# One matmul for the high and low parts of the last 184 tokens in the first input phase

## The reference

```python
h = rmsnorm(x, norm_g)
proj = jnp.einsum('btd,dc->btc', h, w_in)
xa, za, v, bg, cg, zb, ga, gb = jnp.split(proj, SPLIT_IDX, axis=-1)
ya, new_pool = pool_mixer(xa, pool_buf, offset, w_pool_mix, pool_scale)
ya = ya * jax.nn.silu(za)
yc, new_conv = conv_mixer(cg * v, conv_buf, w_conv)
yb = bg * yc * jax.nn.silu(zb)
merged = (jax.nn.sigmoid(ga + b_gate[:D_MODEL]) * jnp.einsum('bte,ed->btd', ya, w_proj_pool)
          + jax.nn.sigmoid(gb + b_gate[D_MODEL:]) * jnp.einsum('bte,ed->btd', yb, w_proj_conv))
x = x + jnp.einsum('btd,de->bte', merged, w_out)
```

## Time and profile before

| | |
|---|---|
| median of 3 runs | 2417.72 us (2416.65 to 2417.8) |
| span of the profiled execution, first to last instruction | 2415.0 us |
| TensorE (PE) matmul busy | 2392.6 us, 99% |
| TensorE weight loads (PEld) busy | 2332.7 us, 97% |
| VectorE (DVE) busy | 1700.3 us, 70% |
| ScalarE (ACT) busy | 894.0 us, 37% |
| granted TensorE clock, mean | 0.998 of full |

### The profile page before, as it was taken

The page is one execution under the profiler, slowest core; times in us unless marked ns, Lnnn a source line. Parts: engine busy times, 40 slices in busy tenths (PEclk is TensorE's granted clock), DMA queues, the critical chain, the costliest instruction groups (busy, mean ns, idle before and its releaser), DMA issues.

```text
span 2415.0 us, 42738 instructions
## 1 busy us (share of the span) xinstructions
PE 2392.6 (99%) x17842; PEld 2332.7 (97%) x17842; DVE 1700.3 (70%) x2329; ACT 894.0 (37%) x1316; POOL 116.0 (5%) x220
## 2 busy tenths in 40 slices
PE   8999999999999999999999999999999999999998
PEld 7999999999999999999999999999999999888886
DVE  6676666666666586777868777765755887877676
ACT  7333333333333343323322222233533533532535
POOL 3010000000000000000000000000000011100000
PEclk9999999999999999999999999999999999999999
DMA  7563333232323454434433343345645767898656
GB/s 268 198 205 110 107 106 111 99 118 90 127 90 127 163 188 151 150 136 151 150 132 113 136 138 135 107 154 208 227 168 171 275 241 278 296 343 306 243 178 227
DMA packets 196655, 418.06 MB, mean 173 GB/s; under 512 B 12617, under 2 KB 114045, under 8 KB 182448
## 3 DMA queue, kind: packets, MB, share of 16 engines
q1 hardware_dynamic: 170928, 284.85, 35.0%
q0 software_dynamic: 23744, 125.24, 13.7%
q10 hardware_dynamic: 1792, 5.24, 0.6%
HBM read 281.00 MB, written 133.77 MB: 172 GB/s over the span
## 4 chain that ended last, share of the span: by engine, by line
PE 97%; DVE 0%; issue 0%; ACT 0%; DVEq 0%; POOL 0%; POOLq 0%; ACTq 0%
PE ps L1328 76%; PE ps L1475 12%; PE ps L1390 7%; PE ps L1497 1%; PE ps L1543 1%; DVE ops L2195 0%; ACT ops L1683 0%; DVE out L2458 0%; PE ps L1520 0%; DVE out L2511 0%; DVEq L226 0%; DVE h0raw L2612 0%; POOL rstd L1309 0%; ACT squares L1804 0%; ACT squares L1813 0%
## 5 line engine op out<-in xcount | busy, mean ns | idle before, releaser
L1328 PE MATMUL ps<-ops,hi 128*128 128x272 f32 x9728 | 1325.2, 288 | 0.1
L1328 PEld LDWEIGHTS ps<-ops,hi 128*128 128x128 f32 x9728 | 1264.5, 188 | 0.4 <-DVE ops L2195 0.3
L1328 PE MATMUL ps<-ops,lo 128*128 128x272 f32 x4864 | 708.6, 288 | 0.0
L1328 PEld LDWEIGHTS ps<-ops,lo 128*128 128x128 f32 x4864 | 647.4, 188 | 0.0
L1604 ACT ACTIVATE hi<-sb 128x512 fp32r<-128x512 f32 x440 | 278.2, 632 | 576.3 <-PE ps L1328 444.1
L2169 DVE TENSOR_TENSOR pb<-pb,ps 128x544 f32<-128x544 f32 x330 | 237.5, 720 | 261.8 <-PE ps L1328 261.6
L2025 DVE TENSOR_TENSOR lo<-sb,hi 128x512 fp32r<-128x512 f32 x440 | 303.1, 689 | 153.3 <-ACT hi L1604 148.7
L1604 ACT ACTIVATE hi<-raw 128x512 fp32r<-128x512 f32 x264 | 166.8, 632 | 371.6 <-PE ps L1328 357.6
L2025 DVE TENSOR_TENSOR lo<-raw,hi 128x512 fp32r<-128x512 f32 x264 | 181.8, 689 | 103.0 <-ACT hi L1604 103.0
L1475 PE MATMUL ps<-ms_hi,mt 128*128 128x512 f32 x896 | 221.3, 389 | 0.0
L1475 PEld LDWEIGHTS ps<-ms_hi,mt 128*128 128x128 f32 x896 | 168.2, 188 | 34.8
(11 more groups left out here) (173 smaller groups left out, 1580.2 us busy)
## 6 DMA issues: line engine op xcount, KB each, us to landing
raw<-in_w_in_dram SPq DMA_DIRECT2D x156, 512.0 KB, 4.0
pb<-part SPq DMA_DIRECT2D x39, 1088.0 KB, 6.0
part<-pb POOLq DMA_DIRECT2D x37, 1088.0 KB, 5.3
mt_raw<-opq SPq DMA_DIRECT2D x28, 1024.0 KB, 6.3
gates<-pb POOLq DMA_DIRECT2D x16, 1088.0 KB, 8.7
gate<-gates SPq DMA_DIRECT2D x32, 544.0 KB, 6.2
ms<-in_w_out_dram SPq DMA_DIRECT2D x16, 1024.0 KB, 9.5
ops_raw<-opq SPq DMA_DIRECT2D x15, 1088.0 KB, 6.8
```

Source lines behind the costliest of these rows:

```text
L1328: mm = nc.tensor.matmul(ps[b][:, c, 0:HC], w[:, w_slot, kt * P:(kt + 1) * P], operand[:, kt, half, c * HC:(c + 1) * HC], start=fresh and k ...
```

## The change

In the products q = 0 to 6 of pairs 3 to 39 (H0 alone, the half-length L products not), the 544 tokens are no longer cut in two quarters of 272. They are cut in 360 (MAIN) and 184 (REST). For each `kt` and the high weights, two matmuls take the 360 tokens (high part, low part) into the same columns, and one takes the high and the low parts of the 184 tokens side by side, 368 columns, into two neighbouring ranges of the accumulator. For the low weights there is one matmul of 360 and one of 184. The first range of 184 lies right behind the 360, so that the read-out sees 544 columns in a row; the second range is added by a further VectorE instruction, `drain_rest`. All slots so made are now counted in `dve_count`, and waits that had named ScalarE's copy alone name both.

```diff
+    def is_wide(g):
+        return NC < g < FIRST[H1]
+
+    def has_rest(s):
+        g, q = pair_of(s)
+        return is_wide(g) and q < NQ
...
-        if by_dve:
+        if by_dve or has_rest(s):
             nd += 1
             dve_count[s] = nd
...
+        REST = 184
+        MAIN = TH - REST
+        EDGE = 512 - MAIN
...
         def psum(s):
+            if has_rest(s):
+                return flat[bank(s)][:, EDGE:EDGE + TH]
             return ps[bank(s)][:, :, 0:HC]
+
+        def psum_rest(s):
+            return flat[bank(s)][:, EDGE + TH:EDGE + TH + REST]
...
+            def wide_terms(b, w_slot, operand, weights, fresh):
+
+                own = flat[b]
+                pe.wait_ge(w_hi, weights)
+                for kt in range(KQ):
+                    w = hi[:, w_slot, kt * P:(kt + 1) * P]
+                    for half in (0, 1):
+                        nc.tensor.matmul(own[:, EDGE:512], w, operand[:, kt, half, 0:MAIN],
+                                         start=fresh and kt == 0 and half == 0, stop=False, skip_group_check=True)
+                    nc.tensor.matmul(own[:, 512:512 + 2 * REST].rearrange("p (h n) -> p h n", h=2), w,
+                                     operand[:, kt, :, MAIN:TH], start=fresh and kt == 0, stop=False,
+                                     skip_group_check=True)
+                pe.wait_ge(w_lo, weights)
+                for kt in range(KQ):
+                    w = lo[:, w_slot, kt * P:(kt + 1) * P]
+                    nc.tensor.matmul(own[:, EDGE:512], w, operand[:, kt, 0, 0:MAIN], start=False, stop=kt == KQ - 1,
+                                     skip_group_check=True)
+                    mm = nc.tensor.matmul(own[:, 512:512 + REST], w, operand[:, kt, 0, MAIN:TH], start=False,
+                                          stop=kt == KQ - 1, skip_group_check=True)
+                mm.then_inc(product_done, 1)
...
-                    terms(bank(s), s % R, ops[:, q], split_of_slot(s), None, q in (0, 1, 5))
+                    wide_terms(bank(s), s % R, ops[:, q], split_of_slot(s), q in (0, 1, 5))
                     return
...
+            def drain_rest(s):
+                g, q = pair_of(s)
+                if s not in dve_count or not has_rest(s):
+                    return
+                own = target(s)[:, MAIN:TH]
+                if s in act_count and not (in_quad(g) and (g, q) == (first_of(g) + 1, 0)):
+                    dve.wait_ge(act_drained, act_count[s])
+                else:
+                    dve.wait_ge(main_drained, main[0])
+                each = nc.vector.tensor_tensor(own, own, psum_rest(s), ALU.add)
+                if in_quad(g) and q == 4:
+                    own = out_tile(g)[:, 1, MAIN:TH]
+                    each = nc.vector.tensor_tensor(own, own, psum_rest(s), ALU.add)
                 each.then_inc(dve_drained, 1)
...
                 split_lo(s + R - 1)
+                drain_rest(s - 1)
                 weight_sum(s + R)
```

More of the change, by code:

```diff
@@ L392, in bank @@
             return k
+        REST = 184
+        MAIN = TH - REST
+        EDGE = 512 - MAIN
+        assert 0 < EDGE and 2 * REST <= 512 and REST % 2 == 0
         def psum(s):
+            if has_rest(s):
+                return flat[bank(s)][:, EDGE:EDGE + TH]
             return ps[bank(s)][:, :, 0:HC]
+        def psum_rest(s):
+            return flat[bank(s)][:, EDGE + TH:EDGE + TH + REST]
         def out_tile(g):
@@ L405, in target @@
                 th, c = divmod(i, 2)
-            return out_tile(g)[:, c, th * TH:(th + 1) * TH].rearrange("p (b n) -> p b n", n=HC)
+            own = out_tile(g)[:, c, th * TH:(th + 1) * TH]
+            return own if has_rest(s) else own.rearrange("p (b n) -> p b n", n=HC)
         def quad_target(s):
@@ L475, in bass_hybrid_stream_step @@
         dve_drained = sem("dve_drained")
+        main_drained = sem("main_drained")
         ops_hi = sem("ops_hi")
@@ L1617, in quad_drain @@
                 elif (g, q) == (a + 1, 0):
-                    dst, src = target(s)[:, 0, :], psum(s)[:, 0, :]
+                    dst, src = target(s)[:, 0:HC], psum(s)[:, 0:HC]
                 else:
@@ L2065, in weight_sum, with add_main @@
                 nc.vector.tensor_tensor(sb_of(g, q), a, b, op).then_inc(s_made, 1)
+            main = [0]
+            def add_main(dst, src):
+                main[0] += 1
+                nc.vector.tensor_tensor(dst, dst, src, ALU.add).then_inc(main_drained, 1)
             def quad_drain(s):
@@ L2070, in quad_drain @@
                 b = a + 1
+                if s in act_count and (g, q) in ((a, 0), (a, 1), (a, 2), (b, 1), (b, 2)):
+                    return
                 after_act = {(a, 3): (a, 2), (a, 4): (a, L2), (a, L0): (a, 0), (a, L2): (a, 0), (a, L3): (a, L2),
-                             (a, L4): (a, L1), (a, L5): (a, L0), (b, 0): (a, L1), (a, L6): (b, 0), (b, 3): (b, 2),
+                             (a, L4): (a, L1), (a, L5): (a, L0), (b, 0): (b, 0), (a, L6): (b, 0), (b, 3): (b, 2),
                              (b, 4): (b, 2)}[g, q]
-                after_dve = {(a, 4): (a, L3), (a, L3): (a, L2), (a, L5): (a, 4), (b, 0): (a, L4), (b, 4): (a, L4)}
+                after_dve = {(a, 3): (a, 2), (a, 4): (a, L3), (a, L2): (a, 0), (a, L3): (a, L2), (a, L5): (a, 4),
+                             (b, 0): (a, L4), (b, 3): (b, 2), (b, 4): (b, 1)}
                 dve.wait_ge(act_drained, act_count[SLOT[after_act]])
@@ L2080, in quad_drain @@
                     own, src = quad_target(s)[:, 0, :], psum(s)[:, 0, :]
+                    nc.vector.tensor_tensor(own, own, src, ALU.add).then_inc(dve_drained, 1)
                 elif q >= NQ:
                     own, src = quad_target(s), psum(s)
+                    nc.vector.tensor_tensor(own, own, src, ALU.add).then_inc(dve_drained, 1)
                 elif (g, q) == (b, 0):
-                    own, src = target(s)[:, 1, :], psum(s)[:, 1, :]
+                    add_main(target(s)[:, HC:TH], psum(s)[:, HC:TH])
                 else:
[L2086 to L2090, removed]
+                    add_main(target(s), psum(s))
+                    if q == 4:
+                        add_main(out_tile(g)[:, 1, 0:TH], psum(s))
+            def drain_rest(s):
+                g, q = pair_of(s)
+                if s not in dve_count or not has_rest(s):
+                    return
+                own = target(s)[:, MAIN:TH]
[7 more added lines that the diff above has]
+                    each = nc.vector.tensor_tensor(own, own, psum_rest(s), ALU.add)
                 each.then_inc(dve_drained, 1)
@@ L2144, in drain @@
                     return
+                if s in act_count:
+                    return
                 c, th = TARGET[q]
@@ L2147, in drain @@
                     if q == 0 and is_kept(g - 1):
-                        dve.wait_ge(act_drained, act_count[SLOT[g - 1, 6]])
-                        dve.wait_ge(dve_drained, dve_count[SLOT[g - 1, 5]])
+                        wait_product_drained(dve, SLOT[g - 1, 6])
                     elif q == 0:
@@ L2154, in drain @@
                 else:
-                    dve.wait_ge(act_drained, act_count[SLOT[g, (2, 1, 0)[q - 3]]])
+                    wait_product_drained(dve, SLOT[g, (2, 1, 0)[q - 3]])
                 dve.wait_ge(product_done, done_of(s))
@@ L2167, in drain @@
                     each.then_inc(dve_drained, 1)
+                elif has_rest(s):
+                    add_main(target(s), psum(s))
                 else:
```

## The result

| | before | after |
|---|---|---|
| median of the runs | 2417.34 us (2416.65 to 2417.8) | 2432.26 us (2431.82 to 2433.13) |
| ratio | | 1.0062, 95% interval 1.0048 to 1.0076 |
| span of the profiled execution | 2415.0 us | 2430.0 us |

The change makes the kernel 14.9 us slower. The forecast was 8.7 us slower, 2426.4 us, range 2418 to 2435.5: the sign and the mechanism hold, the size was off by 6 us.

What follows compares the result with a forecast made beforehand. TensorE's matmul distances were taken to bound the kernel. A step went from 755.0 to 654.6 + 111.5 = 766.1 ns; over 780 steps that is +8.7 us, so 2417.72 + 8.7 = 2426.4 us, range 2418 to 2435.5.

Steps and rivals of the forecast that it cites:

- What bounds: Whole kernel: only the distance between matmul starts on TensorE sets the time; the chain runs along it for 97%.
- 780 steps: Wide products of H0: 195 products with four kt steps each, every step losing one matmul and one weight load.
- The small matmul: Low-weight matmul of 184 columns: bound by the next weight load, 111.5 ns instead of 88.9; the change gains only below 100.4.
- the load doesn't bind: Rival at the matmul of 184 columns: it takes 88.9 ns, so the kernel is faster, 2408.7 us; chance 0.14.
- partly bound: Rival: loads take some 100 ns, or the 360s carry less fixed part; 2417.4 us at 100 ns, no change; chance 0.09.
- The large matmuls: Three of 360 and one of 368 per step: 162.8 and 166.2 ns by a straight line, 654.6 ns together.
- a late tile: Rival in H0's quads: (b, 0) waits for its tile, 4 us more, 2430.4 us; chance 0.13, shared with the load rival.
- VectorE's adds: Second-strip adds in H0: 227 of about 340 ns, 77 us, each taking about 0.255 us of VectorE's time, hidden on average.
- The tightest place: Between (a, 4) and (b, 0), which takes the same tile: 0.12 us left after the new adds, met 16 times.
- The rival that the step is done as two matmuls: Rival at the matmul of 2 x 184: carried out as two, it brings +53 us, 2470.7 us; chance 0.01.
- More than the load: Rival at the small matmul: fixed part on top of the load, 123 ns, 2435.3 us; chance 0.13, shared with late tile.
- The figures from the Trainium skill: For wide products: load 107 ns, 2.5 ns above columns, or 81 ns sustained; the forecast preferred the trace's 111.5 and 11.5 ns.

Runs made afterwards that it cites:

- e9: Changed kernel with each product's four low-weight matmuls of 360 first, then the four of 184: 2430.95 us, ratio 1.0058 to the kernel before.
- the sweep of REST: Changed kernel with REST 128, 192, 232, 240 or 256 in place of 184: 2447.24, 2429.54, 2411.74, 2413.55 and 2412.88 us.
- e1: Changed kernel without VectorE's 227 adds of the second strip and the waits on them, matmuls as changed: 2433.09 us, ratio 1.0067 to the kernel before.
- e5: Kernel before, with the four kt steps of quarter 0 ahead of those of quarter 1 in every product of 24 matmuls: 2409.05 us, ratio 0.9967.
- e3: Changed kernel with the matmul of 368 put between the two high-weight ones of 360: 2431.51 us, ratio 1.0061 to the kernel before.
- e12: Changed kernel with the matmul of 368 reading neighbouring high-part tokens in one piece: 2430.64 us, ratio 1.0055 to the kernel before.

## Why the prediction was right, and what was off

**What bounds.** Right. The chain is TensorE's at 97% before and after, and only distances on it moved the time.

**780 steps.** Right: 780 matmuls and loads fewer.

**The small matmul.** Right in its mechanism, and close in size: 108.3 ns against 111.5. The rows were the better ones: in that trace the first two loads after such a wait start 108 to 110 ns apart. The 111.5 of the earlier trace rows is what small ones in a row take, as e9 shows (111.7). The rival "the load doesn't bind" needed 88.9 ns, "partly bound" some 100; both are out by the sweep of REST. The fast loads of the earlier trace rows (63 ns) were another kind, as their shorter record (139 against 188 ns) said.

**The large matmuls.** This is the step that was mis-sized. They were put on a straight line through 272 and 512 columns with 1 ns of error each. They took 2.1 ns (360, high weights), 2.8 (368) and 4.7 (360, low weights, behind a small one) more: 2 x 2.1 + 2.8 + 4.7 = 11.7 ns a step. With the small one's -3.2 and 0.1 from the six before, that is 8.6 ns a step, 6.7 us; the kernel came out 6.2 us over the forecast. Of the 4.7 a part comes from the small matmul ahead (e9: 3.9 ns came off the 360s when it went, and 2.6 came back on each small one). Two points can't test a line: the sweep shows 10.5 to 17.5 ns above the columns between its ends, where the line had 12.5 to 13.4. Why is open. The prediction named 2 ns off the line as what would make it wrong; that happened, and it went the way the sign already pointed. That 2432.26 us still lies in the range is in part luck: the forecast with its own errors ended at 2432, and the range went on to 2435.5 for a load with the fixed part on top or a late tile, and neither came.

**VectorE's adds.** Right. The groups after show them at the 340 ns that were worked out from the slope of the earlier trace rows:

```profile
L2153 DVE TENSOR_TENSOR pb<-pb,ps 128x184 f32<-128x184 f32 x195 | 66.2, 339 | 0.0
L2156 DVE TENSOR_TENSOR pb<-pb,ps 128x184 f32<-128x184 f32 x32 | 10.8, 339 | 0.0
```

77 us as instructions; VectorE's busy time grew by 56.8, since each starts before the one ahead has ended, as counted. "VectorE is busy near 77 us more" was a slip against that count, which gives 227 x 0.255 = 58.

**The tightest place.** Right: (b, 0) doesn't wait. Timeline after, the quad with a = 26, VectorE after (a, 4), then PE, beside the earlier trace rows:

```profile
606.86 1.35 DVE L2114 TENSOR_TENSOR pb<-pb,ps 128x544 f32<-128x544 f32 x2 [1.75 <-PE ps L1370]
608.13 0.69 DVE L2068 TENSOR_TENSOR lo<-raw,hi 128x512 fp32r<-128x512 f32 x1
608.73 0.34 DVE L2153 TENSOR_TENSOR pb<-pb,ps 128x184 f32<-128x184 f32 x1
608.99 0.34 DVE L2156 TENSOR_TENSOR pb<-pb,ps 128x184 f32<-128x184 f32 x1
609.24 0.68 DVE L2108 TENSOR_TENSOR sb<-raw 128x512 f32<-128x512 f32 x1
...
609.60 0.49 PE L1360 MATMUL ps<-ops,hi 128*128 128x360 f32 x2
```

The second add ends at 609.33, the first load of (b, 0) starts at 609.47 and its first matmul at 609.60. So 0.14 us was left, where 0.12 was forecast. And e1, without any of it, is no faster.

**The rival that the step is done as two matmuls** is out by the count. "More than the load" named the right side, but not the place: the small one took 108.3 ns and not 123, and the large ones took more.

**The figures from the Trainium skill.** In the Trainium skill, "TensorE: Matmul & The Clock Gate", section "LDWEIGHTS (loading the stationary operand)", puts the load at 107 ns; 108.3 ns is the floor that the sweep shows. Section "Back-to-back issue gap" of that page of the Trainium skill has 81 ns for a sustained stream of 128 columns. It does not occur here: with REST 128 such a matmul takes 108.3 ns between large ones, and sixteen in a row are 111 ns apart. Nor is the 2.5 ns above the columns that this section gives for isolated matmuls this kernel's, where 10.5 to 22 ns stand above the columns of those that outlast a load.

## What to carry to other kernels

Merging matmuls can save the fixed part of each that goes (12.5 ns at 272 columns here, of which 6 to 8 a step were had with REST 232 to 256), but only as long as every matmul that is left lasts as long as the load of the next one's weights: put the shortest one's columns beside the distance of two loads in a row before anything else. Where a cut has a free size, choose it so that the shortest matmul is not below the load's length (here REST 232 in place of 184 turned +15 us into -6, about 16 of these 21 us by this). And a price taken from a line between two sizes should carry the error that a third size would show, above all when it is multiplied by hundreds.

## What was not expected of the hardware

- Matmuls of 272 columns in the order of e5 (the same strip and other weights each time) are 125.3 ns apart, and 125.8 in the order of before (the two strips in turn, the same weights twice); over 14592 matmuls this is 8 us. Which of the two differences does it isn't shown; in e3, with 360 and 368 columns and the same weights three times, taking turns between the strips was 1.1 ns a step faster.
- A matmul's fixed part above its columns isn't constant: 12.5 ns at 272, 14 to 17.5 at 352 to 360, 13.4 at 512 in one piece, 22 at 2 x 256. Neither the byte at which the pieces begin (REST 192 and 232) nor the turn of the strips (e3) explains it, and one piece in place of two took 1.8 ns off the 368 (e12). The cause stays open.
- After the change a low-weight matmul of 360 behind a small one takes 169.1 ns, and 162.7 behind the 368. It is no general rule: a high-weight one of 360 takes 165.9 ns behind a small one and 166.0 behind the 368. All of this is by the reading of the loads.
